# Order of the expert items: a 96-row item directly behind the merged round, a 64-row item between the two 96-row items

## Chip, cores and metric

One core of one Trainium2 chip. The metric is the device time of one execution in microseconds (us). Before the change three runs gave a median of 1451.09 us (1450.13 to 1452.8).

## What is computed

The reference is a two-layer transformer on 256 tokens of width 1024. Each layer mixes tokens with three kinds of attention; the first layer has a dense feed-forward part, the second a mixture of eight experts. The change touches only the experts:

```python
def moe_swiglu(x, router_w, w1, w3, w2):
    logits = (x @ router_w).astype(F32)
    top_val, top_idx = lax.top_k(logits, TOP_K)          # TOP_K = 2
    top_w = jax.nn.softmax(top_val, axis=-1)
    gates = jnp.sum(jax.nn.one_hot(top_idx, N_EXPERTS, dtype=F32) * top_w[..., None], axis=-2)
    y = jnp.zeros(x.shape, F32)
    for e in range(N_EXPERTS):                            # 8
        y = y + gates[..., e:e + 1] * swiglu(x, w1[e], w3[e], w2[e]).astype(F32)
    return y.astype(x.dtype)
```

An expert has w1 and w3 (1024 x 3584 each) and w2 (3584 x 1024), all fp32.

## The kernel before

**Items and rounds.** Each token goes to two of the eight experts. The kernel gathers the rows of one expert into an *item* with room for 64, 96 or 128 rows. In the profiled execution there are eight items, one for each expert. They run in the order of the table `ORDER` (line 62): `s0` (64 rows), the merged round `both` with its two members `ms` (64) and `mb` (128), then `s2` (64), `w1` (96), `w2` (96), one pass of a loop named `small` (64), and `last` (64). `AFTER` and `BEFORE` (lines 64 and 65) name the neighbour of each round. Which expert an item takes is looked up in a table on the chip by `ITEM_OF` (line 68), which doesn't depend on the order.

**One item.** The 3584 hidden columns are taken in seven blocks j (NJ = 7). For a block TensorE multiplies the gathered rows by two loads of w1 (`up`, "A"), turns the gated product of the block before (`turn`, line 2833), multiplies by two loads of w3 ("B") and then by two loads of w2 for the block before (`down`, "C"). A load is 128 x 2048 fp32, 1024 KB. So an item needs 7 x 6 = 42 loads, and eight items 336, which is the sum of the three `in_experts` counts in part 6 of the page (144 + 144 + 48). The loads are the same in number and size whatever the rows of the item; only TensorE's time for one load differs: `small_products` (line 2794) for 64 rows, `wide_products` (lines 2808 and 2810) for 96, `full_products` (line 2801) for 128.

**The joint of two rounds.** In the last block of a round `gather` (line 2752) collects the rows of the next item. Behind that block stand A of block 0 of the next item, the last turn and C of this round, B of block 0 of the next item, and then the scatter (`scattered`, line 2881), which adds the result of this round to the residual and uses no load. In ScalarE's program the gathered rows are copied out of PSUM (line 1456) into a buffer that belongs to the row count; if the round that ends has an item of the same row count, `gathered` waits first until that round's last B is done (lines 1462 to 1466).

**The ring of loads.** The queue on SyncE (SP) issues all loads in the order of use (`load`, line 966). They go into a ring of 14 slots (`ITEM_RING`). Load n may be issued only when TensorE has finished with load n - 14: for half of them that is signalled by a semaphore of its own (`s_used`), for the rest by the count of filled PSUM tiles. Behind the experts four loads of `in_stream` (weights of the last gate) follow on the same queue, and with them the kernel's end.

Of the kernel before, what the change touches and what calls it, by code (L numbers as in the profile page):

```python
# [58 lines left out]
NI = NE + MORE  # L59
WHOLE0 = NS + MORE  # L60
STATIC, RUN, LAST = 1, 2, 3
ORDER = ("first", "s0", "both", "s2", "w1", "w2", "small", "last")
MEMBERS = {name: (name,) for name in ORDER} | {"both": ("ms", "mb")}
AFTER = {"first": "s0", "s0": "both", "both": "s2", "s2": "w1", "w1": "w2", "w2": "small", "small": "small"}
BEFORE = {"s0": "first", "both": "s0", "s2": "both", "w1": "s2", "w2": "w1", "small": "small", "last": "small"}
ROUND_OF = {member: name for name in ORDER for member in MEMBERS[name]}
ROWS = {"w1": WIDE, "w2": WIDE, "mb": P}
ITEM_OF = {"s0": 0, "ms": 1, "s2": 2, "w1": WHOLE0, "w2": WHOLE0 + 1, "mb": NI - 1}
# [228 lines left out]
def begun(name, i):  # L297
    return f"{name}+{i}"


def member_of(ph):
    if "+" not in ph:
        return ph
    name, i = ph.split("+")
    return MEMBERS[AFTER[name]][int(i)]

# [5 lines left out]
def whole_now(ph):  # L312
    return rows_now(ph) > HALF


def own(ph, j):
    if j:
        return ph
    name = ROUND_OF[ph]
    return begun(BEFORE[name], MEMBERS[name].index(ph))  # L320

# [12 lines left out]
def next_members(name):  # L334
    return list(enumerate(MEMBERS[AFTER[name]])) if name in AFTER else []

# [10 lines left out]
def gather_tiles(t, name):  # L347
    for i, member in gathered_whole_first(name):
        for half in range(2 if whole_now(member) else 1):
            alone = len(MEMBERS[AFTER[name]]) == 1  # L350
            t.add(("GA", begun(name, i), half), (7, 3)[half] if alone or whole_now(member) else 2, "a")
# [21 lines left out]
def round_tiles(t, name):  # L373
    members = MEMBERS[name]
    for j in range(1, NJ):
        for ph in members:
            t.add(("A", ph, j), 0, "a")
            if j == WEIGHED:
                t.add(("GT", ph), 7, "a")
            t.add(("TT", ph, j - 1), 6, "v")  # L380
            if j == NJ - 1 and ph == members[-1]:
                gather_tiles(t, name)
            t.add(("B", ph, j), 1, "v")
    for i, _ in next_members(name)[:1]:
        t.add(("A", begun(name, i), 0), 0, "a")
    for ph in members:
        t.add(("TT", ph, NJ - 1), 6, "v")
        for m in range(2 if whole_now(ph) else 1):
            t.add(("YY", ph, m), result_bank(ph, m), "av" if ph == "last" else "a")
    for i, _ in next_members(name):  # L390
        if i:
            t.add(("A", begun(name, i), 0), 0, "a")
        t.add(("B", begun(name, i), 0), 1, "v")
    if name != "last":
        for ph in members:
            scatter_tiles(t, ph)


def plan_tiles():
# [21 lines left out]
    t.begin(STATIC)  # L421
    for name in ORDER[1:-2]:
        round_tiles(t, name)
# [9 lines left out]
def plan_loads(tiles):  # L433
# [61 lines left out]
    turns, rounds = list(order), {}  # L495
    for name in ORDER[1:]:
        start = early[0]
# [87 lines left out]
def build(nc, x, stream, experts, columns, rows, final_w, consts, out):  # L585
    tiles = plan_tiles()[0]
    plan = plan_loads(tiles)
    n_before, per_load = len(plan["turns"]), len(plan["rounds"]["small"])
    static = plan["turns"] + [key for name in ORDER[1:-2] for key in plan["rounds"][name]]
    n_run = len(static)  # L590
# [39 lines left out]
    with ExitStack() as ctx:  # L630
# [312 lines left out]

        rounds_before = {name: min(n, ORDER.index("small") - 1) for n, name in enumerate(ORDER[1:])}

# [94 lines left out]
        def _(pool):  # L1040
# [104 lines left out]
            def places_of_next(name, items, now=None):  # L1145

                pool.wait_ge(s_weigh, through(rounds_before[name] + 1, now, "items"))
                pause(62)
                for i, item in enumerate(items):
                    ins = nc.gpsimd.tensor_copy(now_place[i], item_table[:, bass.ds(item, 1), :])  # L1150
                ins.then_inc(s_place, 1)
                pool.drain()
# [9 lines left out]
            for name in ORDER[1:-2]:  # L1162
                places_of_next(name, [LOOPED if member == "small" else ITEM_OF[member] for member in MEMBERS[AFTER[name]]])
            pool.wait_ge(s_tab, 1)
# [1892 lines left out]
```

## Time and profile before

| | us |
|---|---|
| median of three runs | 1451.09 |
| the profiled execution | 1450.37 |
| its span | 1448.5 |
| TensorE busy | 1400.7 (97%) |
| DMA, mean over the span | 314 GB/s |

The page divides the span into 40 slices of 36.2 us; the experts fill slices 15 to 38. A window of the trace gives for a stretch the busy time of each engine, TensorE's granted clock (1.00 is full speed), the share of the 16 DMA engines' time, and the GB/s that they moved. A timeline gives start, length, engine, line, operation, and in brackets how long the engine was idle before and what ended it. SPq is SyncE's queue; a long SPq time of an issue means that the issue itself was held up.

### The profile page before, as it was taken

Reading aid. Unit: us, or ns where it says so; the run is one execution under the profiler, and the core shown is the slowest. Engines: PE = TensorE matmul, PEld = TensorE weight load, DVE = VectorE, ACT = ScalarE, POOL = GpSimd, SP = SyncE. Lnnn points to the kernel's source line nnn. Section 1 sums busy time; section 2 is a strip of 40 time slices with the busy share of each in tenths; the row PEclk is TensorE's granted clock in tenths of the full one; section 3 lists DMA queues with packets and bytes.
Section 4 is the critical chain, followed back from the end, with each engine's and each line's share of the span. In section 5 each row is a group of like instructions: output and inputs, shape, how many; then the busy total and the mean of one; then the engine's idle time right before and its main releaser. Section 6 shows DMA issues by size and latency. Waiting matters only on the chain.

```text
span 1448.5 us, 29882 instructions
## 1 busy us (share of the span) xinstructions
PE 1400.7 (97%) x13080; PEld 1042.9 (72%) x13080; DVE 514.1 (35%) x878; ACT 385.1 (27%) x628; POOL 133.2 (9%) x175
## 2 busy tenths in 40 slices
PE   9999999999999999999999999999999999998867
PEld 8999899999899987554333343568998997554425
DVE  5987765556689774201000001001101001001024
ACT  7656543334665844010000000000000001000015
POOL 2663000000027500000000000000000000000001
PEclk9999999999999999999999999999999999999998
DMA  8562345545544519999999999999999999999990
GB/s 352 194 175 112 117 177 195 203 181 189 208 170 157 166 38 422 421 421 420 421 420 421 420 421 388 395 421 419 419 419 419 399 398 371 406 420 421 421 385 30
DMA packets 81233, 454.50 MB, mean 314 GB/s; under 512 B 16336, under 2 KB 25936, under 8 KB 27088
## 3 DMA queue, kind: packets, MB, share of 16 engines
q1 hardware_dynamic: 80816, 451.00, 78.1%
q8 instruction: 104, 1.70, 0.5%
q0 software_dynamic: 288, 1.59, 0.3%
q14 instruction: 25, 0.20, 0.0%
HBM read 447.96 MB, written 4.60 MB: 312 GB/s over the span
## 4 chain that ended last, share of the span: by engine, by line
PE 83%; DMA 9%; SPq 3%; DVE 3%; ACT 1%; issue 1%; POOL 0%; DVEq 0%; ACTq 0%
PE ps L2794 18%; PE ps L2801 10%; PE ps L2810 10%; PE ps L2324 8%; PE ps L2326 7%; PE ps L2325 7%; PE ps L2808 6%; DMA raw<-in_experts 4%; DMA raw<-in_stream 3%; SPq L966 3%; DMA upper<-in_experts 2%; PE ps L2331 2%; PE ps L2332 2%; PE ps L2335 2%; PE ps L2833 1%; PE ps L2881 1%
## 5 line engine op out<-in xcount | busy, mean ns | idle before, releaser
L1478 ACT ACTIVATE work<-ps 128x256 f32<-128x256 f32 (+2 forms) x56 | 24.5, 437 | 704.6 <-PE ps L2794 406.3
L908 DVE TENSOR_TENSOR wlo<-raw,whi 128x2048 fp32r<-128x2048 f32 x85 | 198.0, 2352 | 26.3 <-ACT whi L904 26.3
L2324 PE MATMUL ps<-xh,whi 128*128 128x256 f32 x656 | 186.8, 285 | 0.0
L1997 DVE COPY attn<-ps 128x256 f32<-128x256 f32 (+2 forms) x56 | 27.5, 491 | 446.8 <-PE ps L2833 446.8
L2326 PE MATMUL ps<-xh,wlo 128*128 128x256 f32 x656 | 183.8, 280 | 0.0
L2325 PE MATMUL ps<-xl,whi 128*128 128x256 f32 x656 | 183.7, 280 | 0.0
L2794 PE MATMUL ps<-raw,attn 128*64 128x256 f32 (+1 forms) x1200 | 173.2, 426 | 10.3 <-DMA raw<-in_experts 6.9
L2794 PE MATMUL ps<-upper,attn 128*64 128x256 f32 (+1 forms) x1200 | 171.4, 423 | 8.2 <-DMA upper<-in_experts 8.1
L904 ACT CAST whi<-raw 128x2048 fp32r<-128x2048 f32 x85 | 160.5, 1909 | 2.3 <-DMA raw<-in_stream 2.3
L2794 PEld LDWEIGHTS ps<-upper,attn 128*64 128x64 f32 x1200 | 84.6, 137 | 83.2 <-issue 30.2
L2794 PEld LDWEIGHTS ps<-raw,attn 128*64 128x64 f32 x1200 | 83.1, 137 | 85.1 <-issue 44.8
L2003 DVE TENSOR_TENSOR work<-work,ps 128x256 f32<-128x256 f32 (+2 forms) x56 | 27.3, 487 | 293.0 <-PE ps L2794 154.8
L2324 PEld LDWEIGHTS ps<-xh,whi 128*128 128x128 f32 x656 | 123.5, 188 | 1.4
L2325 PEld LDWEIGHTS ps<-xl,whi 128*128 128x128 f32 x656 | 123.5, 188 | 0.9
L2326 PEld LDWEIGHTS ps<-xh,wlo 128*128 128x128 f32 x656 | 123.4, 188 | 0.0
L2808 PE MATMUL ps<-raw,attn 128*32 128x384 f32 x864 | 99.6, 487 | 1.3 <-DVE attn L1997 1.3
L2810 PE MATMUL ps<-raw,attn 128*32 128x128 f32 x864 | 100.6, 273 | 0.0
L2810 PE MATMUL ps<-upper,attn 128*32 128x128 f32 x864 | 100.2, 273 | 0.0
L2808 PE MATMUL ps<-upper,attn 128*32 128x384 f32 x864 | 99.2, 486 | 0.0
L2810 PEld LDWEIGHTS ps<-upper,attn 128*32 128x32 f32 x864 | 94.3, 110 | 0.0
L2810 PEld LDWEIGHTS ps<-raw,attn 128*32 128x32 f32 x864 | 93.0, 110 | 0.0
L2801 PE MATMUL ps<-raw,attn 128*32 128x512 f32 x576 | 65.4, 594 | 1.4 <-DVE attn L1997 0.8
(393 smaller groups left out, 2000.6 us busy)
## 6 DMA issues: line engine op xcount, KB each, us to landing
raw<-in_experts SPq DMA_DIRECT2D x144, 1024.0 KB, 21.6
upper<-in_experts SPq DMA_DIRECT2D x144, 1024.0 KB, 21.8
raw<-in_stream SPq DMA_DIRECT2D x85, 1024.0 KB, 5.4
work<-in_experts SPq DMA_DIRECT2D x48, 1024.0 KB, 21.6
m_rows<-work SPq DMA_DIRECT2D x2, 768.0 KB, 4.1
work<-x_inv_rows SPq DMA_DIRECT2D x2, 768.0 KB, 5.5
work<-xt_rows SPq DMA_DIRECT2D x2, 768.0 KB, 7.1
cst<-in_consts SPq DMA_DIRECT2D x1, 1195.5 KB, 13.3
```

The lines of the kernel that those rows point to most:

```text
L904: nc.scalar.copy(upper_slot(n), landed_slot(n)).then_inc(s_hi, 1)
L908: nc.vector.tensor_tensor(lower_slot(n), landed_slot(n), upper_slot(n).bitcast(F32), ALU.subtract).then_inc(s_lo, 1)
L966: sp.dma_start(landed_slot(n), src).then_inc(s_land[slot_of(n)], 16)
L2324: pe.matmul(out, ah, bh, start=start, stop=False)
L2325: pe.matmul(out, ah, bl, start=False, stop=False)
L2326: return pe.matmul(out, al, bh, start=False, stop=stop)
L2331: pe.matmul(out, xu, wu, start=start, stop=False)
L2332: return pe.matmul(out, xd, wu, start=False, stop=False)
L2794: ins = pe.matmul(bank(key, 0, width)[HALF * side:HALF * side + HALF], rows, w[:, width * side:width * side + width], start=start, stop=stop)
L2801: ins = pe.matmul(bank(key)[GROUP * g:GROUP * g + GROUP], rows[:, GROUP * g:GROUP * g + GROUP], w, start=start, stop=stop)
L2808: pe.matmul(bank(key, 0, 384)[GROUP * g:GROUP * g + GROUP], rows(g), w[:, 0:384], start=start, stop=stop)
L2810: ins = pe.matmul(bank(key, P * g, P)[WIDE:P], rows(g), w[:, 384:512], start=start and g == 0, stop=stop and g == 2)
```

## The change

Three tables are rewritten. `ORDER`, `AFTER` and `BEFORE` now have `w1` behind `both`, then `s2`, then `w2`. Nothing else is edited. All plans (PSUM banks, semaphore counts, the order of loads, the programs of the five engines) are derived from these tables.

```diff
-ORDER = ("first", "s0", "both", "s2", "w1", "w2", "small", "last")
+ORDER = ("first", "s0", "both", "w1", "s2", "w2", "small", "last")
 MEMBERS = {name: (name,) for name in ORDER} | {"both": ("ms", "mb")}
-AFTER = {"first": "s0", "s0": "both", "both": "s2", "s2": "w1", "w1": "w2", "w2": "small", "small": "small"}
-BEFORE = {"s0": "first", "both": "s0", "s2": "both", "w1": "s2", "w2": "w1", "small": "small", "last": "small"}
+AFTER = {"first": "s0", "s0": "both", "both": "w1", "w1": "s2", "s2": "w2", "w2": "small", "small": "small"}
+BEFORE = {"s0": "first", "both": "s0", "w1": "both", "s2": "w1", "w2": "s2", "small": "small", "last": "small"}
```

The first place is TensorE's program at the end of `both`. L2752 is the gather of the next item, L2801 is `mb` (128 rows), L2794 is an item of 64 rows, L2833 a turn. Before:

```order
3166 L2752 MATMUL ps<-work,hn 64x64 x32
3167 L2801 MATMUL ps<-raw,attn 32x512 x16
3168 L2801 MATMUL ps<-upper,attn 32x512 x16
3169 L2801 MATMUL ps<-work,attn 32x512 x32
3170 L2794 MATMUL ps<-raw,attn 64x256 x8
3171 L2794 MATMUL ps<-upper,attn 64x256 x8
3172 L2833 MATMUL ps<-cst,work 128x128 x2
```

And with the change:

```order
3166 L2752 MATMUL ps<-work,hn 64x96 x32
3167 L2801 MATMUL ps<-raw,attn 32x512 x16
3168 L2801 MATMUL ps<-upper,attn 32x512 x16
3169 L2801 MATMUL ps<-work,attn 32x512 x32
3170 L2808 MATMUL ps<-raw,attn 32x384 x3
3171 L2810 MATMUL ps<-raw,attn 32x128 x3
```

The gather now takes 96 rows, and A of the next item is that of a 96-row item (lines 2808 and 2810, eight pairs for each of its two loads), where two loads of 64-row work stood. B of the next item changes in the same way ahead of the scatter.

The second place is ScalarE's program from the gather at the end of `both` on, where one row stands for one kind of work: L1456 copies the gathered rows of the next item (64 or 96 wide), L1478 is the activation of a block (256 wide for 64 rows, 384 for 96), L1492 copies the results of a 96-row item. Before:

```order
331 L1456 ACTIVATE attn<-ps,cols 128x64 x8
335 L1478 ACTIVATE work<-ps 128x256 x3
338 L1456 ACTIVATE attn<-ps,cols 128x96 x8
341 L1478 ACTIVATE work<-ps 128x384 x3
344 L1456 ACTIVATE attn<-ps,cols 128x96 x8
350 L1478 ACTIVATE work<-ps 128x384 x3
353 L1456 ACTIVATE attn<-ps,cols 128x64 x8
```

And with the change:

```order
331 L1456 ACTIVATE attn<-ps,cols 128x96 x8
335 L1478 ACTIVATE work<-ps 128x384 x3
338 L1456 ACTIVATE attn<-ps,cols 128x64 x8
344 L1478 ACTIVATE work<-ps 128x256 x3
347 L1456 ACTIVATE attn<-ps,cols 128x96 x8
350 L1478 ACTIVATE work<-ps 128x384 x3
353 L1456 ACTIVATE attn<-ps,cols 128x64 x8
```

The row counts run 64, 96, 96 before and 96, 64, 96 now; the number of instructions is the same on every engine, and the programs of GpSimd and of SyncE are the same row for row, since the expert of each load is read from the table.

## Rows read from the trace of the kernel before

**Rows 1.** The page, part 2: the span in 40 slices.

```profile
PE   9999999999999999999999999999999999998867
PEclk9999999999999999999999999999999999999998
GB/s 352 194 175 112 117 177 195 203 181 189 208 170 157 166 38 422 421 421 420 421 420 421 420 421 388 395 421 419 419 419 419 399 398 371 406 420 421 421 385 30
```

**Rows 2.** Windows from round end to round end: us, busy times, PEclk, DMA share, GB/s.

```profile
677.35:902.53 225.18, 222.84 (x1905) 85.96 (x1903) 22.07 (x41) 10.32 (x26) 0.32 (x2) 1.00 1.01 419
902.53:987.91 85.38, 84.86 (x777) 50.38 (x776) 8.36 (x21) 5.73 (x17) 0.32 (x2) 1.00 0.98 401
987.91:1110.00 122.09, 121.44 (x2117) 115.94 (x2119) 12.44 (x24) 8.15 (x24) 0.32 (x2) 1.00 1.01 419
1110.00:1228.15 118.15, 117.35 (x1984) 109.05 (x1984) 11.34 (x23) 7.83 (x24) 0.32 (x2) 1.00 0.99 391
1228.15:1309.22 81.07, 80.46 (x648) 43.73 (x649) 8.09 (x21) 5.36 (x17) 0.00 (x0) 1.00 1.01 414
1309.22:1405.90 96.68, 78.32 (x522) 36.49 (x520) 8.27 (x18) 5.03 (x9) 0.00 (x0) 1.00 1.01 421
```

**Rows 3.** Waits of TensorE from 902.5 to 1309 us, the whole answer.

```profile
PE ps L2808 <- DVE attn L1997: 1.3, 2, 0.7
PE ps L2794 <- DVE attn L1997: 1.0, 2, 0.5
```

**Rows 4.** SyncE's queue at the end of `both`.

```profile
893.37 0.33 SPq L966 DMA_DIRECT2D raw<-in_experts  x1
895.12 0.34 SPq L966 DMA_DIRECT2D upper<-in_experts  x1
904.98 0.33 SPq L966 DMA_DIRECT2D raw<-in_experts  x1
```

**Rows 5.** TensorE's timeline at the end of `both`.

```profile
893.01 1.90 PE L2794 MATMUL ps<-upper,attn 128*64 128x256 f32 x16
894.84 1.13 PE L2881 MATMUL ps<-work 64*128 64x512 f32 x4
...
902.53 1.95 PE L2794 MATMUL ps<-raw,attn 128*64 128x256 f32 x16
```

**Rows 6.** Expert loads, issue to landing: windows 912 to 985, then 1130 to 1225 us.

```profile
DMA to landing us min/median/max: 10.0/21.9/29.6
...
DMA to landing us min/median/max: 6.1/7.9/11.0
```

**Rows 7.** Shorter windows, columns as in Rows 2.

```profile
902.50:912.50 10.00, 10.00 (x79) 5.64 (x80) 1.53 (x3) 0.38 (x1) 0.00 (x0) 1.00 0.73 246
912.50:1015.00 102.50, 101.98 (x1183) 71.10 (x1183) 10.22 (x23) 6.33 (x18) 0.32 (x2) 1.00 1.01 421
1015.00:1110.00 95.00, 94.35 (x1641) 89.58 (x1636) 9.04 (x18) 7.17 (x22) 0.32 (x2) 1.00 1.01 419
1243.50:1386.00 142.50, 128.28 (x968) 65.73 (x966) 12.20 (x30) 6.86 (x21) 0.00 (x0) 1.00 1.01 421
```

**Rows 8.** TensorE's timeline in `last`, with its waits.

```profile
1382.48 1.95 PE L2794 MATMUL ps<-raw,attn 128*64 128x256 f32 x16 [0.64 <-DMA raw<-in_experts]
1384.88 1.95 PE L2794 MATMUL ps<-upper,attn 128*64 128x256 f32 x16 [0.45 <-DMA upper<-in_experts]
1386.76 0.44 PE L2833 MATMUL ps<-cst,work 128*128 128x128 f32 x2
1388.80 1.95 PE L2794 MATMUL ps<-work,attn 128*64 128x256 f32 x16 [1.61 <-DMA work<-in_experts]
```

**Rows 9.** The chain that ended last, from 1380 us on.

```profile
1378.40 27.66 DMA raw<-in_stream
```

**Rows 10.** ScalarE's copies of gathered rows for `s2` and for `w2`, and TensorE behind the first.

```profile
867.92 1.75 ACT L1456 ACTIVATE attn<-ps,cols 128x64 f32<-128x64 f32 x8 [8.95 <-PE ps L2801]
...
1083.94 1.96 ACT L1456 ACTIVATE attn<-ps,cols 128x96 f32<-128x96 f32 x8 [8.10 <-PE ps L2810]
...
874.65 1.95 PE L2794 MATMUL ps<-raw,attn 128*64 128x256 f32 x16
```

**Rows 11.** Page, part 3: the queue that fetches instructions, and its share.

```profile
q8 instruction: 104, 1.70, 0.5%
```

## Prediction

> **What bounds the kernel now.** I read the page's slices first. The change can only act between slice 24 and the end. There TensorE is 90% busy or more in all slices but the last four, and the GB/s are either 419 to 422 or lower [rows 1]. The higher figure is the stream of expert loads running freely. The end of the kernel hangs on that stream: the chain that ended last comes out of the last gate weights, which land at 1378.40 + 27.66 = 1406.06 us, behind all expert loads on the same queue [rows 9], and in `last` TensorE waits for one load after the other [rows 8]. So a microsecond in which the stream stands still and isn't made up is a microsecond of time, and the stream can't make up: its rate has one upper value.
>
> Next I read the windows by round [rows 2]. An item is 42 loads of 1.0486 MB, 44.04 MB; at 421 GB/s that is 104.6 us. TensorE takes 85.4 us for `s2`, 122.1 us for `w1`, 118.2 us for `w2`. The difference of 3.9 us between the two wide rounds lies in what a round does for the next one: `w1` gathers 96 rows and does A and B of block 0 of a wide item, `w2` does them for a 64-row item. In all of 902.5 to 1309 us TensorE never waits for a load, only 2.3 us for VectorE [rows 3]. So TensorE is late there, the stream is ahead, and what stops the stream is the ring: load n goes out when load n - 14 has been used.
>
> That the ring is full at the end of `both` is seen directly. SyncE issues nothing between 895.12 and 904.98 us [rows 4], the time in which TensorE does the scatter, which frees no slot; the next issue follows the first A load of `s2`, which TensorE begins at 902.53 us [rows 5]. The 10 us behind 902.5 have 246 GB/s [rows 7]. That it is full again in `w2` is seen in the time from issue to landing: a median of 7.9 us between 1130 and 1225 us, a nearly empty DMA queue to which loads come one by one, against 21.9 us in `s2`, where many issued loads stand in line [rows 6]. The rate says the same: 419 GB/s in `w1`, 391 in `w2` [rows 2].
>
> **The balance before.** Count how far the stream is behind the point at which the ring is full (its *room*, in us of stream). After `both` the room is 0. `s2` frees slots faster than the stream fills them: room 104.6 - 85.4 = 19.2. `w1` frees slower: 19.2 - (122.1 - 104.6) = 1.7. `w2` would take 118.2 - 104.6 = 13.6 more; 1.7 is there, so the stream is stopped for 11.9 us. As a cross-check from the rates, 118.15 x (1 - 391/421) is 8.4 us in `w2`, and 81.07 x (1 - 414/421) is 1.3 us in `small`, where the stop that `w2` left is served out, with 0.6 in `w1`: 10.3 us, near enough, as the instruction fetches are counted as moved bytes.
>
> **The change, step by step.** TensorE's work is the same in sum: `both` grows by the 3.9 us, since it now gathers and starts a wide item, the first wide item ends in 118.2 us, as `w2` does, because a 64-row item follows; `s2` keeps its 85.4 us (a wide item still follows), `w2` its 118.2 us. 3.9 + 118.2 + 85.4 + 118.2 is the 325.6 us from before (85.4 + 122.1 + 118.2), within rounding. TensorE should reach the end of `w2` at 1228 us as before.
>
> The stream:
> - `both`: the ring is full, so its 3.9 us more are lost in full.
> - `w1`: the ring is full from its first load on, so the whole excess of 13.6 us is lost.
> - `s2`: room 19.2 us.
> - `w2`: takes 13.6 of it. Nothing is lost, and 5.6 us of room are left.
>
> The room that is left is the price. Before, the stream stood at the ring's limit when `w2` ended; now it stands 5.6 us behind it, with the same TensorE time on the clock. (By losses: 3.9 + 13.6 = 17.5 against 11.9.) A room that stands empty before the last two light items has no use, as those are bound by the stream anyway. **First term: +5.6 us.**
>
> The second term is small pauses of the stream. While the ring is the limit, a pause of the stream costs nothing; in free stretches each is paid. Before, `s2` and `w1` ran free and their pauses were swallowed by the stop in `w2`. Now `s2` and `w2` run free and nothing behind them swallows anything. What such a pause is shows in `last`: one wait of 1.61 us where the pattern has 0.45 to 0.65 [rows 8], so about 1.0 us, once in some 97 us with 522 matmuls [rows 2]. The nearest cause in the page is the queue that fetches instructions, with 0.5% of the DMA time [rows 11]. `s2` and `w2` have 777 + 1984 = 2761 matmuls [rows 2]. If pauses go by instructions, that makes 2761/522 x 1.0 = 5.3 us, the upper bound; if they go by mean share, 0.5% of 203.5 us, 1.0 us, the lower. The free stretches before show 421 and 419 GB/s [rows 7], which is nearer to the lower end, though the mean over 16 DMA engines hides a delay of one of them, for which a load must still wait. I take 2.5 us. **Second term: +2.5 us (1.0 to 5.3).**
>
> Waits at the joints: before, ScalarE's copy of the gathered rows waits for the last B where the row counts meet (`both` to `s2`, `w1` to `w2`) [rows 10]. With the change no neighbours share a buffer, so these waits of 8.95 and 8.10 us go. The copies for `s2` ended at 869.7 us, 5 us ahead of the matmuls that need them at 874.65 us, and TensorE shows no wait for ScalarE [rows 3]. I put this at 0. The two waits for VectorE's turned copy, 0.5 to 0.7 us for each joint, stay with each joint. GpSimd's and SyncE's programs don't change.
>
> Sum: 5.6 + 2.5 = 8.1 us on the profiled execution's 1450.37 us, 1458.5 us; that execution is 0.7 us under the median of the runs, so the median becomes 1451.1 + 8.1 = **1459.2 us**.
>
> **Rivals.**
>
> *The stream isn't stopped by the ring, but slowed by wide matmuls* (no change). If 96-row work itself slowed the DMA, by contention for memory, its loss would go with the items and not with their order, and the time would stay at 1451, give or take 2. For it speaks that the low rates stand in a wide round. Against it: `w1` has the same matmuls at 419 GB/s as `w2` at 391 [rows 2], and SyncE's issues wait for TensorE [rows 4, 6]. It also stands for a mixture in which less than half of my first term is real.
>
> *The shared buffers were the wait* (faster). If the copies behind `gathered` hold up TensorE in a way that isn't in the records, both joints gain, and since the ring is full there, a gain of TensorE is a gain of the stream. The most is 8.95 + 8.10 = 17 us, less the 8.1: 1442 us. It decides only if TensorE wins more than 8.1 us at the joints; the rows show 0 waits for ScalarE and 2.3 us of waits in all.
>
> *The clock falls in `small`* (much slower). The stream arrives 8 us later, so TensorE starts to wait for loads earlier, in the second half of `small`. In `last` TensorE is busy 78.32 of 96.68 us at a clock of 1.00, 2.4 GHz, with waits of 0.45 to 1.61 us [rows 2, 8]. If the clock went to 1.2 GHz for the whole of `last`, its 78.3 us would be 156.6, some 60 us over the stream: 1519 us. The rows speak against it, as the waits keep their size and only become more.
> The Trainium skill (TensorE: Matmul & The Clock Gate, "Why this matters for your kernels") advises to avoid idle gaps of TensorE between bursts of matmuls, since they bring the clock down; by that page this change would be the wrong direction beyond my sum, but the trace has such waits at full clock [rows 8].
>
> *TensorE runs dry in `s2`.* From a full ring `s2` uses up 19.2 us plus the pauses. It did so before from the same state without one wait for a load [rows 3]; and a wait there would cost nothing, with 5.6 us of room unused behind it.
>
> **How the numbers follow.** Forecast 0.80; no change 0.12; faster 0.03; clock or another new wait 0.05. 0.2% of this kernel, 2.9 us, is about what a measurement can tell from no change. The forecast's own bounds are 5.6 + 1.0 and 5.6 + 5.3, 1457.7 to 1462.0; a first term smaller by half, 1454, is where the forecast goes over into the no-change case. To hold 8 in 10, with the bounds of my reading of the ring, I give 1454 to 1463. Slower: 0.80 + 0.05 = 0.85; same 0.12; faster 0.03.
>
> **What would show it.** Right: `both` ends at about 906.5 us and the first wide round at about 1024.6; that round has a rate near 44.04 MB / 118.2 us = 373 GB/s and an issue-to-landing time of some 8 us; `w2` ends at 1228 us again, but at 419 to 421 GB/s with long issue-to-landing times; TensorE's first wait for a load comes in `small`, not in `last`; the last gate weights land near 1414 us. Wrong: a rate above 400 in the first wide round (the ring wasn't full), a rate under 405 in `w2` (contention), `w2` ending well before 1228 us (joints), a clock under 1.00 before the last landing.

## The result, and the profile after

| | before | changed |
|---|---|---|
| median, us | 1451.26 | 1461.81 (4 runs, 1459.83 to 1463.28) |
| ratio | 1 | 1.0067, 95% interval 1.0049 to 1.0086 |
| profiled execution, us | 1450.37 | 1459.83 |
| its span, us | 1448.5 | 1458.0 |

The change makes the kernel slower by 10.6 us in the medians and by 9.5 us between the two profiled executions. In a second comparison (`changed_again` below) the median was 1460.5 against 1451.2, ratio 1.008 (1.0062 to 1.0098). The ratios here and below are given as recorded; they differ by up to 0.2% from the quotient of the two medians.

The page's slices of the changed kernel, as in [rows 1]:

```profile
PE   9999999999999999999999999999999999988867
PEclk9999999999999999999999999999999999999998
GB/s 355 195 184 93 120 199 196 180 174 202 207 169 168 138 87 422 421 421 421 421 420 421 420 421 312 380 378 364 399 422 419 420 418 421 420 421 421 420 375 29
```

Before, two light dips (388 395) followed the merged round and a second group (399 398 371) stood in `w2`. Now there is one deep hole in slices 24 to 28 (312 380 378 364 399), and from slice 29 on nothing but 418 to 422 as long as experts are loaded. The stream of loads is held back in one stretch, from the end of the merged round to the end of the first wide round, and never again.

The windows by round (`both` from 674.68 to 907.33, then `w1`, `s2`, `w2`, `small`), to be held against [rows 2]. The first of them begins with the scatter of `s0`, the one in [rows 2] 1.9 us later, behind that scatter; from the same point `both` takes 230.73 us (676.60 to 907.33) against 225.18:

```profile
674.68:907.33 232.65, 230.30 (x2043) 94.23 (x2039) 23.70 (x43) 10.76 (x26) 0.32 (x2) 0.99 1.00 410
907.33:1025.31 117.98, 117.33 (x1984) 109.09 (x1983) 11.23 (x22) 7.85 (x24) 0.32 (x2) 1.00 0.94 363
1025.31:1110.70 85.39, 84.87 (x779) 50.30 (x778) 8.38 (x21) 5.75 (x17) 0.32 (x2) 1.00 1.00 412
1110.70:1228.90 118.20, 117.40 (x1986) 109.10 (x1984) 12.38 (x25) 7.86 (x24) 0.32 (x2) 1.00 1.01 419
1228.90:1319.96 91.06, 83.12 (x648) 43.31 (x649) 8.09 (x21) 5.37 (x17) 0.00 (x0) 1.00 1.01 421
```

TensorE takes 118.0, 85.4 and 118.2 us for the three rounds, within 0.2 us of what the prediction took from before. `w2` ends at 1228.90 us; it was 1228.15. The rates are those of a full ring in `w1` (363 GB/s) and of a free stream in `w2` (419, where 391 stood before).

The time from issue to landing shows the same. This is the changed kernel from 912 to 1020 us (`w1`), and then from 1130 to 1225 us (`w2`), to be held against [rows 6]:

```profile
DMA to landing us min/median/max: 5.3/6.5/8.3
...
DMA to landing us min/median/max: 18.8/23.7/26.8
```

The order of the two figures is turned round: the nearly empty DMA queue now stands in the first wide round, the long line in the second.

TensorE's first waits for loads behind the merged round, in `small` (changed kernel, timeline):

```profile
1275.12 1.95 PE L2794 MATMUL ps<-upper,attn 128*64 128x256 f32 x16 [0.45 <-DMA upper<-in_experts]
1277.00 0.44 PE L2833 MATMUL ps<-cst,work 128*128 128x128 f32 x2
1278.92 1.95 PE L2794 MATMUL ps<-raw,attn 128*64 128x256 f32 x16 [1.48 <-DMA raw<-in_experts]
```

From 907 to 1275 us there is none; before the change TensorE went from 902.5 to 1309 us without one [rows 3], and the first came at 1315 us. TensorE catches up with the stream some 40 us earlier, because the stream is behind. And the chain ends on the last gate weights later than in [rows 9]:

```profile
1389.47 26.29 DMA raw<-in_stream
```

That is 1415.76 us against 1406.06, +9.7 us. The whole difference of the spans (9.5) is in the landing of these weights.

One more thing happened in this execution, apart from the ring. During the scatter of `mb`, at the end of `both`, TensorE's granted clock fell. The windows of 1 us from 902 to 906 us:

```profile
902.00:903.00 1.00, 0.97 (x2) 0.63 (x3) 0.48 (x1) 0.00 (x0) 0.00 (x0) 0.70 1.01 426
903.00:904.00 1.00, 1.00 (x2) 0.34 (x2) 0.23 (x1) 0.00 (x0) 0.00 (x0) 0.50 0.92 385
904.00:905.00 1.00, 1.00 (x2) 0.29 (x1) 0.45 (x1) 0.00 (x0) 0.00 (x0) 0.50 0.16 66
905.00:906.00 1.00, 1.00 (x3) 0.34 (x1) 0.53 (x1) 0.00 (x0) 0.00 (x0) 0.60 0.00 0
```

A clock of 0.50 is 1.2 GHz. From about 902.4 to 905.8 us TensorE had half its clock, and the eight matmuls of this scatter took 5.37 us, against 3.86 us before the change and in the second profile of the changed kernel. That is 1.5 us of the 10.5 us.

For the experiments one measure is of use that leaves out everything ahead of the experts: the time from the start of the first gather (line 2752, or further down where an edit adds lines) to the landing of the last gate weights. I call it the *expert part*. Before: 562.18 to 1406.06, 843.9 us. Changed: 561.33 to 1415.76, 854.4 us. It is needed, since five of the profiled executions reach the experts 4 to 9 us later than the others, because of what happens in the first 80 us of the span, where nothing was edited (last section).

### The profile page after: what moved, and what is told of

Read it like the earlier page. It is cut to its first block, busy times and chain, and to the rows that moved or that the text cites. A ratio compares the mean times of both kernels' runs of the same rounds, so it can differ in the third digit from the quotient of the medians.

```text
span 1458.0 us, 29880 instructions
## 1 busy us (share of the span) xinstructions
PE 1404.2 (96%) x13080; PEld 1042.8 (72%) x13080; DVE 513.1 (35%) x878; ACT 385.5 (26%) x628; POOL 131.5 (9%) x175
## 4 chain that ended last, share of the span: by engine, by line
PE 80%; DMA 11%; SPq 5%; DVE 2%; ACT 1%; issue 1%; POOL 0%; DVEq 0%; ACTq 0%
PE ps L2794 15%; PE ps L2801 10%; PE ps L2810 10%; PE ps L2324 8%; PE ps L2326 7%; PE ps L2325 7%; PE ps L2808 6%; DMA raw<-in_experts 5%; SPq L966 5%; DMA raw<-in_stream 3%; DMA upper<-in_experts 2%; PE ps L2331 2%; PE ps L2332 2%; PE ps L2335 2%; PE ps L2881 1%; PE ps L2833 1%
## 5 line engine op out<-in xcount | busy, mean ns | idle before, releaser
L1478 ACT ACTIVATE work<-ps 128x256 f32<-128x256 f32 (+2 forms) x56 | 24.5, 438 | 729.4 <-PE ps L2794 414.8
L2794 PE MATMUL ps<-raw,attn 128*64 128x256 f32 (+1 forms) x1200 | 173.4, 426 | 14.1 <-DMA raw<-in_experts 10.8
L2794 PE MATMUL ps<-upper,attn 128*64 128x256 f32 (+1 forms) x1200 | 171.8, 424 | 12.1 <-DMA upper<-in_experts 12.1
L2794 PEld LDWEIGHTS ps<-upper,attn 128*64 128x64 f32 x1200 | 83.9, 137 | 89.2 <-DMA upper<-in_experts 28.6
L2794 PEld LDWEIGHTS ps<-raw,attn 128*64 128x64 f32 x1200 | 83.5, 136 | 88.5 <-issue 45.2
L2801 PE MATMUL ps<-raw,attn 128*32 128x512 f32 x576 | 65.4, 594 | 1.4 <-DVE attn L1997 0.8
```

The source lines that it names most:

```text
L2794: ins = pe.matmul(bank(key, 0, width)[HALF * side:HALF * side + HALF], rows, w[:, width * side:width * side + width], start=start, stop=stop)
L2801: ins = pe.matmul(bank(key)[GROUP * g:GROUP * g + GROUP], rows[:, GROUP * g:GROUP * g + GROUP], w, start=start, stop=stop)
```

## Experiments: where the light item stands

Four orders were run, with nothing edited but the same three tables. The orders named here are those between `s0` and `small`. Two theories were held against each other, besides a slowing by wide matmuls: that the unused room of the ring is the price, or that the joint of `both` with a 96-row item is.

**`both, w1, w2, s2`.**

```diff
-ORDER = ("first", "s0", "both", "s2", "w1", "w2", "small", "last")
+ORDER = ("first", "s0", "both", "w1", "w2", "s2", "small", "last")
```

> Order both, w1, w2, s2, small, last: the 64-row item stands behind both wide ones; nothing else differs. Theory (room of the ring): the ring is full at the end of w2, then s2 opens 104.6 - 85.4 = 19.2 us of room that nothing uses before the stream-bound end. First term +19.2, and 1 to 3 for the longer joint behind both and for pauses in the free stretch of s2: 1451 + 20 to 22 = 1471 to 1473. Rival joint (the price is the joint of both with a 96-row item, as in the changed kernel): the same joint once, so +8 to +10, 1460. Rival contention (wide matmuls slow the stream wherever they stand): 1451.

Measured: 1475.31 us, ratio 1.0142 (1.0107 to 1.0177), 2 us above the expected range. Expert part 568.44 to 1434.92, 866.5 us, +22.6 us. The joint is the same as in the changed kernel, and the price more than twice as high. TensorE's waits for loads in this kernel from 907 to 1320 us:

```profile
PE ps L2794 <- DMA upper<-in_experts: 6.1, 13, 0.5
PE ps L2794 <- DMA raw<-in_experts: 5.8, 12, 0.6
PE ps L2794 <- DMA work<-in_experts: 2.2, 4, 0.6
```

14 us of waits for loads, all of them in `small` (from 1235 us on), where there was none before [rows 3]: the room that `s2` opens turns into idle time of TensorE, as nothing heavy is left to use it.

The expected size was too small for a reason that the trace shows. The 85.4 us, and with them the room of 19.2 us, hold for an `s2` that gathers and starts a wide item. Here a 64-row item follows. The beginning of `s2` and that of `small`:

```profile
1152.93 1.95 PE L2794 MATMUL ps<-raw,attn 128*64 128x256 f32 x16
...
1233.69 1.95 PE L2794 MATMUL ps<-raw,attn 128*64 128x256 f32 x16
```

So `s2` takes 80.8 us, and its room is 104.6 - 80.8 = 23.8 us. The +22.6 us measured are nearly all of it.

**`s2, both, w1, w2`.**

```diff
+ORDER = ("first", "s0", "s2", "both", "w1", "w2", "small", "last")
```

> Order s2, both, w1, w2, small, last. Theory (room of the ring): s0 leaves the ring empty of landed loads, so s2 is bound by the stream and TensorE waits some 19 us in it; both, w1, w2 follow without a light item between, the ring is full from the end of both on and the whole excess 17.5 + 13.6 is lost. The 19.2 us of s2 are never used as room: +19 to 22, 1470 to 1473, though the room that is left at the end of w2 is 0. Joint: +8 to 10, 1460. Contention: 1451.

Measured: 1475.75 us, ratio 1.0158 (1.0121 to 1.0195), 3 us above the expected range; expert part 562.48 to 1430.26, 867.8 us, +23.9 us. TensorE's waits in `s2`, 680 to 775 us, show where the room went:

```profile
PE ps L2794 <- DMA upper<-in_experts: 5.4, 12, 0.5
PE ps L2794 <- DMA raw<-in_experts: 2.7, 6, 0.7
PE ps L2794 <- DVE work L2003: 2.5, 4, 0.6
PE ps L2794 <- DMA work<-in_experts: 2.3, 2, 1.9
```

10.4 us of waits for loads, two light items in a row; some 19 us were expected. The waits listed are not the whole loss, as the lengths of the rounds show. `s0` and `s2` end together here:

```profile
781.68 1.99 PE L2881 MATMUL ps<-work 64*128 64x512 f32 x8
783.60 3.67 PE L2794 MATMUL ps<-work,attn 128*64 128x256 f32 x32
```

From the first gather at 562.48 us that is 221.1 us. Before, `s0` took 115.2 us with the same joint to `both` (562.18 to 677.35), and an `s2` that starts a 64-row item takes 80.8 us (`s2_last`), 196.0 us together. So 25.1 us are lost in these two rounds, near the 23.8 us that such an `s2` would open as room. The light item costs nearly the same ahead of all heavy work as behind it. A room can't be opened further than to the point at which TensorE has nothing to work on.

**`w1, both, s2, w2`.**

```diff
+ORDER = ("first", "s0", "w1", "both", "s2", "w2", "small", "last")
```

> Order w1, both, s2, w2, small, last. Theory (room of the ring): the end is that of the changed kernel (s2 opens 19.2 us, w2 uses 13.6, 5.6 stay unused), so it takes the time of the changed kernel less what its longer joint costs: +6 to +9, 1457 to 1461. Joint: both is followed by a 64-row item as before, so no price, 1451. Contention: 1451.

Measured: 1458.37 us, ratio 1.0037 (1.0022 to 1.0053); expert part 563.12 to 1414.27, 851.2 us, +7.3 us. This order ends like the changed kernel but has no wide item behind `both`. Most of the price is there all the same, so the joint isn't its cause. By medians, from different comparisons, the changed kernel is 2 to 3.5 us slower than this one; but the profile of the changed kernel without the fall of the clock in the scatter (`changed_again`) has an expert part of 851.4 us, 0.2 us from this one. So the joint costs next to nothing.

**`w1, w2, s2, both`.**

```diff
+ORDER = ("first", "s0", "w1", "w2", "s2", "both", "small", "last")
```

> Order w1, w2, s2, both, small, last: two wide items in a row again, and the merged round ends the heavy part. Theory (room of the ring): s2 opens 19.2 us and both with its excess of 225 - 209 = 16 us and its long scatter uses nearly all of it, so 0 to 3 us of room stay unused: 1451 to 1455. Joint: 1451. Contention: 1451.

Measured: 1450.29 us, ratio 0.9988 (0.9969 to 1.0007); expert part 562.29 to 1404.57, 842.3 us, -1.6 us. The order differs from before in every place, has two wide items in a row, and takes the same time: the heavy part ends with a full ring, as before (SyncE issues no load between 1220.19 and 1229.68 us, while TensorE does the scatter of `mb`). It is the best of the orders tried, and not measurably better than the kernel before.

The four together: with 0, 0, 5.6, 5.6, 23.8 and 23.8 us of room of `s2` unused (`both_last`, before, `w1_first`, changed, `s2_last`, `s2_first`), the expert part is 842.3, 843.9, 851.2, 854.4 (851.4 in the second profile), 866.5 and 867.8 us. The rival that wide matmuls slow the stream falls: the matmuls are the same in all six, 13080 in each profile.

## Experiments: 4.6 us of TensorE work, in five places

The turn of one round got six more transposes, whose results are overwritten by the right ones. Only the name of the round and the order differ between the five kernels:

```diff
+PAD = 3
...
+                for _ in range(PAD if ph == "s2" else 0):
+                    for q in range(2):
+                        pe.transpose(bank(("TT", ph, j), P * q, P), mg[buffer_of(ph, j)][:, P * q:P * q + P], ident)
                 for q in range(4 * rows_now(ph) // P):
```

What it costs TensorE is seen in the turns of `s2` in `pad_before`, the added transposes first, the kernel's own behind them:

```profile
906.14 0.87 PE L2835 MATMUL ps<-cst,work 128*128 128x128 f32 x6
906.85 0.38 PE L2837 MATMUL ps<-cst,work 128*128 128x128 f32 x2
917.65 0.87 PE L2835 MATMUL ps<-cst,work 128*128 128x128 f32 x6
```

A block takes 917.65 - 906.14 = 11.51 us; before it was 10.86. Seven times 0.65 is 4.6 us.

The unedited changed kernel stood beside them:

> The changed kernel itself, for a firmer interval beside the next three. All theories: 1459 to 1462.

Measured: 1460.5 us; expert part 563.05 to 1414.45, 851.4 us, 3.0 us less than in the first profile. 1.5 us of this is one place, the scatter of `mb`. Here is the first profile of the changed kernel, then `changed_again`:

```profile
902.03 5.37 PE L2881 MATMUL ps<-work 128*128 128x512 f32 x8 [0.28 <-DVE h L1896]
...
903.74 3.86 PE L2881 MATMUL ps<-work 128*128 128x512 f32 x8 [0.27 <-DVE h L1896]
```

The eight matmuls took 5.37 us there, at the lower clock, and 3.86 us here, at 1.00, as in the profiles of all the other runs. The waits for VectorE beside them are the same in both (0.77 us ahead of the matmuls of `ms`, 0.28 and 0.27 us here), so they don't tell why the clock fell in one of them. The other 1.5 us lie between the end of `s2` and the landing (307.0 us from the scatter on, against 305.5 here and 305.4 in `w1_first`); where exactly isn't shown. So two profiles of the changed kernel differ by 3 us in the expert part. Below, a pad is held against both: 851.4 us, and 854.4 us or, less the lost clock, 852.9 us.

**In `s2`, order before** (ring full later on, in `w2`):

> The kernel before, with six more transposes in each of the seven turns of s2 (about 0.66 us each time, 4.6 us of TensorE in all; their results are overwritten). Theory (room of the ring): the room is used up by w1 and w2, so every us taken from s2's room is lost in w2: +4.6, 1455.7 (4 to 5). Rival (TensorE isn't the bound in s2, since the stream runs free there): 0, 1451.

Measured: 1455.1 us, ratio 1.0028 (1.0016 to 1.004); expert part 562.09 to 1410.10, 848.0 us, +4.1 us. The work stands where the stream runs free, and is paid almost in full.

**In `s2`, changed order**:

> The changed kernel with the same six more transposes in each turn of s2. Theory (room of the ring): 5.6 us or more of the room are unused at the end of w2, so the 4.6 us cost nothing: 0 against the changed kernel (at most 1). Rival (TensorE's work is what counts in both orders): +4.6 as in the other order.

Measured: 1460.18 us against 1460.5; expert part 569.35 to 1422.51, 853.2 us, between the 851.4 and 854.4 us without it. The same work in the same item costs nothing by the medians and at most 1.8 of its 4.6 us by the profiles.

**In `w1`, changed order** (ring full):

> The changed kernel with six more transposes in each of the seven turns of w1 (4.6 us of TensorE). Theory (room of the ring): the ring is full all through w1, so each us is lost: +4.6 against the changed kernel, 1464 to 1466. Rival (only the number of free slots at the end counts, wherever the work stands): 0, as for the same work in s2.

Measured: 1463.96 us, 3.5 us over `changed_again`, which ran in another comparison (the kernel before: 1451.6 us in this one, 1451.2 in that); expert part 566.82 to 1424.17, 857.4 us, 6.0 us over `changed_again` and 4.5 us over the first profile less its lost clock. Paid.

**In `w2`, changed order**:

> The changed kernel with the same 4.6 us of TensorE in w2. Theory (room of the ring): w2 ends with over 5.6 us of room unused, so 0 to 1 against the changed kernel. Rival (a wide round is bound by TensorE in either order): +4.6.

Measured: 1463.05 us (1459.46 to 1468.01), which by the median is 2.5 us over `changed_again` and would lie between the two expectations. The expert part says 0 to 1: 567.08 to 1419.53, 852.5 us, between the two profiles without it. Its profiled execution, 1463.51 us, has its extra time ahead of the experts, where its clock fell (last section). The recorded mean clocks show that this is what moved the median: four of the seven executions have 0.990 to 0.992, like the profiled one, and the three with 0.994 or 0.995 took 1459.46, 1460.85 and 1461.71 us. Not paid.

**In `small`, order before**:

> The kernel before with the same 4.6 us of TensorE in small, behind the last place where the ring is full. Theory (room of the ring): small opens some 20 us of room that nothing uses, so 0 to 1: 1451 to 1452. Rival (before, TensorE is the bound to the end): +4.6.

Measured: 1451.75 us, ratio 1.0 (0.9985 to 1.0015); expert part 563.17 to 1407.10, 843.9 us, the same as before. Not paid.

So a microsecond of TensorE is paid up to the last point at which the ring is full (the end of `w2` before, the end of `w1` in the changed order) and not behind it.

## Experiments: the shared buffers, and the pauses

**Own buffers** for the gathered rows of `s2` and `w2`, in the order before:

```diff
+        own_rows = {name: attn[:, at:at + KC * n].rearrange("p (k s) -> p k s", s=n) for name, n, at in (("s2", HALF, 3584), ("w2", WIDE, 2560))}
...
-                    dst = x_rows_of[rows_of_item(member)]
-                    if not waited and any(rows_of_item(ph) == rows_of_item(member) for ph in MEMBERS[name]):
+                    dst = own_rows.get(member, x_rows_of[rows_of_item(member)])
+                    if member not in own_rows and not waited and any(rows_of_item(ph) == rows_of_item(member) for ph in MEMBERS[name]):
...
-                        rows = x_rows_of[count][:, k, :]
+                        rows = own_rows.get(member_of(ph), x_rows_of[count])[:, k, :]
```

> The kernel before with gathered rows of s2 and of w2 in buffers of their own, so that ScalarE's copies no longer wait for the last B of the round (8.95 and 8.10 us of wait). Order unchanged. Theory (room of the ring): TensorE never waited for these copies, so 0, 1451. Rival (the shared buffers were the wait): faster by up to 17 us, and by over 2.9 us at least.

Measured: 1450.97 us, ratio 0.999 (0.9975 to 1.0005); expert part 570.15 to 1414.23, 844.1 us, +0.2. ScalarE's copies at the two joints now follow the gather:

```profile
869.12 1.74 ACT L1457 ACTIVATE attn<-ps,cols 128x64 f32<-128x64 f32 x8 [1.93 <-PE ps L2753]
...
1085.48 1.03 ACT L1457 ACTIVATE attn<-ps,cols 128x96 f32<-128x96 f32 x4 [1.41 <-PE ps L2753]
```

The waits of 8.95 and 8.10 us for the last B [rows 10] are gone, at no gain. The rival of the shared buffers falls.

**More instructions on GpSimd**, in the changed order:

```diff
+            def fill(times):
+                for n in range(times):
+                    at, c = 32 * (n % 4), n // 4 % 384
+                    ins = nc.gpsimd.tensor_tensor(scores[at:at + 1, 4 * T + c:4 * T + c + 1], area("rs", 32, 1)[at:at + 1],
+                                                  area("rs", 33, 1)[at:at + 1], ALU.add)
...
+                if name in ("s2", "w2"):
+                    fill(650)
...
+            fill(1600)
             rstd(5)
```

> The changed kernel with 2900 more GpSimd instructions of one element (650 before the places of s2's and of w2's follower, 1600 behind the loop), on an engine that is idle there; their results are used by nobody. Theory (pauses of the stream come from instruction fetches and are paid where the stream runs free): s2 and w2 have 5522 TensorE instructions and 2 to 3 pauses, so 2900 more over s2, w2, small and last bring 1 to 2 pauses of 1.0 to 1.3 us: +1 to +3 against the changed kernel. Rival (the pauses have another cause): 0.

Measured: 1594.48 us. This time decides nothing, as the experiment was built badly. GpSimd's timeline:

```profile
970.08 159.26 POOL L1148 TENSOR_TENSOR scores<-work 1x1 f32<-1x1 f32 x650 [0.16 <-issue]
...
1173.56 399.99 POOL L1148 TENSOR_TENSOR scores<-work 1x1 f32<-1x1 f32 x1600 [0.33 <-issue]
```

One such instruction took 0.25 us from start to start, so the 1600 ran to 1573.5 us and the last norm (`rstd(5)`), which stands behind them, began at 1573.6 us, where it began at 1427.4 in the changed kernel, 146 us late.

The stream of loads doesn't wait for that norm, so the expert part can still be read. It begins at 562.88 us, and ScalarE takes up the last gate weights as they land:

```profile
1416.12 1.90 ACT L904 CAST whi<-raw 128x2048 fp32r<-128x2048 f32 x1 [0.56 <-DMA raw<-in_stream]
```

That is 853.2 us, against 851.4 and 854.4 us (852.9 less the lost clock) without the 2900 instructions: between nothing and 1.8 us more, where the theory asked for 1 to 3. The queues that fetch instructions moved little more: part 3 of the page has 104 and 47 packets, against 104 and 25 in the changed kernel, 0.19 MB in addition. So the experiment shows that 2900 more instructions cost the stream less than 2 us; whether they cost it anything, and whether pauses of the stream come from such fetches, stays open.

## Why the prediction was right, and what was off

The direction, the mechanism and the size held: 1459.2 us was forecast within 1454 to 1463, 1461.81 and 1460.5 us were measured. The clock was not as forecast, and the second term has the right size with a cause that isn't shown.

- *The ring is full behind `both` and in `w2`; the stream has no other reserve.* Right. The rate of the first wide round was put at 373 GB/s and is 363, as the stop that `both` left behind runs on into this window (8 GB/s from 908 to 910 us). Issue to landing: some 8 us forecast, 6.5 measured.
- *TensorE's sum doesn't change.* Right but for 0.75 us at the end of `w2`, which comes from the scatter of 5.37 us at the lower clock (+1.5) and an earlier start of the experts (-0.85).
- *First term, +5.6 us of unused room.* Right, and the best supported step: the six orders follow it, `s2_last` and `s2_first` with the room counted for the item that really follows `s2`, and the pad of 4.6 us in `s2` is paid before and fits into the unused room in the changed order. `w1_first`, whose room is the same without the longer joint, measures +6.9 us by medians.
- *Second term, +2.5 us for pauses.* The size was near enough, and its cause was only argued. Expert parts of 851.4 and 854.4 us are +7.5 and +10.5 us; less 5.6, that leaves 1.9 and 4.9 us, and less the 1.5 us of the lost clock in the second of them, 1.9 to 3.4 us. Most of the smaller figure needs no single pauses. The balance took the 421 GB/s of all queues for the loads. The DMA view of `changed_again` from 1040 to 1240 us, nearly all of it `s2` and `w2` in the free stream, gives the queue of the loads (q1) and one of those that fetch instructions (q8) apart:

```profile
q1 hardware_dynamic: 11485, 83.64, 100.6%
q8 instruction: 21, 0.34, 0.7%
```

83.64 MB in 200 us are 418.2 GB/s, so an item takes 105.3 us and not 104.6. An estimate with this figure: 2 x 105.3 - 203.6 = 7.0 us of unused room, where +7.5 (`changed_again`) and +7.3 (`w1_first`) were measured. That leaves 0.5 us or less in these two for pauses and the joint, and some 2 us in the first profile, which isn't explained. The attempt to raise the number of pauses did not show them.
- *The joints cost nothing.* Right (`own_rows`).
- *The clock stays up.* Right for `small` and `last`: the clock of `small` is 1.00, though waits of up to 1.48 us came. Wrong as a whole: the prediction named a clock under 1.00 before the last landing as a sign against it, and in the first profile that is what is seen, 0.50 from 903 to 905 us. It shows as 0.99 in the window of `both`, while the page's PEclk, in tenths, has a 9 for that slice as for the others. It cost 1.5 us, and the prediction had put the clock at nothing. That this comes from the new order isn't shown: `changed_again` and the pads in the changed order, with the same joint, don't have it in their profiles.
- *The small miss.* The median moved by 10.6 us in one comparison and 9.3 in the other where 8.1 were forecast. In the profiled execution 1.5 us is the fall of the clock in the scatter. It may be frequent: leaving out the executions with 0.991 or less, five of the seven of the changed kernel have a recorded mean clock of 0.993, and only 2 of 43 of the kernel before in the three later comparisons, all others 0.994 or more. But `pad_changed`, with the same joint, has 0.994 or 0.995 in all five of its own, so this isn't settled.

No version beats the kernel before: the best order tried is equal to it.

## What to carry to other kernels

A stream of loads behind a ring that is full loses every microsecond that the consumer takes too long, and gets nothing back for the microseconds that it is quick later on. So keep a balance per stage, consumer time less stream time, with the consumer's time for the neighbour that the stage really has (`s2` takes 85.4 us ahead of a wide item and 80.8 ahead of a small one), and look at what is left of the ring's room at the last heavy stage: a light stage pays for heavy ones only if it stands where the ring has been filled and heavy work still follows. To learn whether an engine's microsecond counts at a place, put 5 us of idle work there and measure, and compare executions with the same mean clock.

## What was not expected of the hardware

TensorE's granted clock fell in 5 of 14 profiled executions, of kernels of either order, far ahead of the experts. The windows 40 to 50, 50 to 60, 60 to 70 and 70 to 80 us of `pad_changed`, whose profiled execution took 1467.98 us, and then the same of `changed_again`, 1458.70 us:

```profile
40.00:50.00 10.00, 10.00 (x87) 10.00 (x87) 9.86 (x13) 5.52 (x6) 5.47 (x5) 1.00 0.66 256
50.00:60.00 10.00, 9.10 (x77) 8.90 (x75) 9.86 (x24) 5.70 (x11) 3.29 (x3) 1.00 0.60 210
60.00:70.00 10.00, 9.53 (x52) 9.56 (x53) 9.07 (x4) 7.03 (x7) 10.00 (x5) 0.61 0.32 107
70.00:80.00 10.00, 10.00 (x64) 9.65 (x65) 4.65 (x18) 2.66 (x4) 4.10 (x8) 0.70 0.28 105
...
40.00:50.00 10.00, 10.00 (x87) 10.00 (x87) 9.86 (x13) 5.53 (x7) 5.29 (x5) 1.00 0.78 274
50.00:60.00 10.00, 9.80 (x83) 9.60 (x81) 9.86 (x24) 6.45 (x11) 3.34 (x3) 1.00 0.57 203
60.00:70.00 10.00, 9.58 (x82) 9.48 (x83) 9.93 (x8) 7.30 (x9) 10.00 (x5) 1.00 0.31 107
70.00:80.00 10.00, 10.00 (x91) 9.62 (x90) 9.77 (x24) 4.78 (x7) 4.10 (x8) 1.00 0.77 207
```

The program is the same up to there. In the one the clock stands at 0.61 and 0.70 on average, that is at 1.2 GHz for more than half of that time, and TensorE completes 52 and 64 matmuls instead of 82 and 91. Ahead of it, from 50 to 60 us, TensorE was busy 9.10 of 10 us, in the other 9.80; its one wait for VectorE between 30 and 80 us was 1.4 us long there and 0.6 us here. But that is not what decides. The kernel before was busy for 9.14 us, `both_last` for 8.88, with waits of 1.3 and 1.7 us, and both kept a clock of 1.00; `pad_w1_changed` was busy for 9.57 us and waited 0.9 us, and its clock fell, to 0.50 by 63 us. The waits of `pad_changed`, `changed_again`, `both_last` and `pad_w1_changed`:

```profile
PE ps L2418 <- DVE work L1679: 1.4, 1, 1.4
...
PE ps L2417 <- DVE work L1678: 0.6, 1, 0.6
...
PE ps L2417 <- DVE work L1678: 1.7, 1, 1.7
...
PE ps L2418 <- DVE work L1679: 0.9, 1, 0.9
```

The first gather starts at 569.35 us in the one and at 563.05 in the other, so it costs 6.3 us, two thirds of what this change does; in the five executions with the fall that gather starts at 566.8 to 570.2 us, in the nine others at 561.3 to 563.2. In `small` and `last` there were waits of 1.48 and 1.61 us at a clock of 1.00. So neither the length of a wait nor the busy time ahead of it tells when the clock falls; its cause is not shown.
